# Gates of a product-key layer by one matmul per token, in groups of seven, with the low part added on VectorE

## The reference, cut to what matters

```python
best, pos = lax.top_k(cand, PEER_TOPK)
idx = jnp.take_along_axis(cand_idx, pos, axis=-1)
g = jax.nn.softmax(best, axis=-1)
u = expert_u[idx]
v = expert_v[idx]
a = jax.nn.gelu(jnp.einsum('td,thkd->thk', xb, u))
return jnp.einsum('thk,thkd->td', (g * a.astype(jnp.float32)).astype(v.dtype), v)
```

## Time and profile before

| | us |
|---|---|
| median of 3 runs | 4504.23 |
| lowest and highest | 4500.32, 4510.47 |
| the profiled execution | 4510.6 |
| its span on the core | 4508.9 |

### The profile page before, as it was taken

How to read it: one execution, slowest core, us unless ns; L and a number is a source line. 1 busy time by engine, 2 the same in 40 slices (tenths; PEclk the granted TensorE clock), 3 DMA queues, 4 the chain that set the end, 5 groups by cost and what they waited for, 6 DMA issues and landing times.

```text
span 4508.9 us, 79330 instructions
## 1 busy us (share of the span) xinstructions
PE 4158.0 (92%) x29440; PEld 3943.4 (87%) x29440; DVE 2733.9 (61%) x4379; ACT 1362.8 (30%) x2001; POOL 1002.1 (22%) x793
## 2 busy tenths in 40 slices
PE   4997988899999999999959979798999999999997
PEld 1785888899999999999838769798999999899997
DVE  1246547966766526777623565478667664277776
ACT  2221233233333333333222113332333333223332
POOL 0035000000122205555200630000001221245551
PEclk8998999999999999999979989999999999999998
DMA  4242221354445558999624422214444545589993
GB/s 142 98 114 107 85 80 61 94 164 136 125 170 180 187 185 309 343 346 341 231 94 131 108 100 83 71 66 135 140 136 147 173 171 204 166 316 349 346 350 147
DMA packets 304236, 781.05 MB, mean 173 GB/s; under 512 B 36352, under 2 KB 159616, under 8 KB 301488
## 3 DMA queue, kind: packets, MB, share of 16 engines
q1 hardware_dynamic: 187344, 483.65, 32.2%
q10 hardware_dynamic: 69600, 154.15, 9.3%
q0 software_dynamic: 47104, 141.00, 8.9%
HBM read 655.79 MB, written 122.88 MB: 173 GB/s over the span
## 4 chain that ended last, share of the span: by engine, by line
PE 80%; DVE 10%; DMA 3%; issue 3%; ACT 2%; another core or an unknown queue 1%; SPq 0%; DVEq 0%; ACTq 0%
PE pg L1318 16%; PE pg L1321 15%; PE pg L1319 15%; PE pm L1353 4%; PE pg L1566 4%; PE pg L1567 4%; PE pm L1567 4%; PE pg L1568 4%; PE pm L1568 4%; PE pm L1566 4%; PE pm L1527 4%; DMA raw<-stream 3%; DVE ys L1001 2%; DVE w_lo L842 1%
## 5 line engine op out<-in xcount | busy, mean ns | idle before, releaser
L1318 PE MATMUL pg<-a_hi,w_hi 128*128 128x260 f32 x6400 | 1706.5, 287 | 128.8 <-DVEq L873 40.6
L1319 PE MATMUL pg<-a_lo,w_hi 128*128 128x260 f32 x6400 | 1686.3, 285 | 0.0
L842 DVE TENSOR_TENSOR w_lo<-raw,w_hi 128x1024 fp32r<-128x1024 f32 x688 | 859.2, 1250 | 1306.2 <-ACT w_hi L751 750.3
L1318 PEld LDWEIGHTS pg<-a_hi,w_hi 128*128 128x128 f32 x6400 | 1226.7, 192 | 147.5 <-issue 110.7
L1321 PE MATMUL pg<-a_hi,w_lo 128*128 128x260 f32 x6400 | 1303.3, 286 | 0.5 <-issue 0.5
L1319 PEld LDWEIGHTS pg<-a_lo,w_hi 128*128 128x128 f32 x6400 | 1223.5, 191 | 0.4
L1321 PEld LDWEIGHTS pg<-a_hi,w_lo 128*128 128x128 f32 x6400 | 1000.4, 191 | 0.0
L751 ACT CAST w_hi<-raw 128x1024 fp32r<-128x1024 f32 x504 | 529.2, 1050 | 803.0 <-PE pm L1568 632.3
L500 POOL DMA_INDIRECT rows<-stream,at_v x256 | 280.5, 1096 | 829.0 <-issue 464.6
L549 ACT ACTIVATE hid<-pg 128x260 f32<-128x260 f32 x512 | 170.4, 385 | 956.7 <-PE pg L1321 953.2
L510 POOL TENSOR_TENSOR one_j<-one_j,g_lo 128x1024 fp32r<-128x1024 f32 x98 | 185.9, 1897 | 1080.9 <-DVEq L1221 1080.9
(11 more groups left out here) (221 smaller groups left out, 5856.1 us busy)
## 6 DMA issues: line engine op xcount, KB each, us to landing
raw<-stream SPq DMA_DIRECT2D x784, 512.0 KB
hidden_dram<-hid SPq DMA_DIRECT2D x256, 196.0 KB, 3.4
gate_dram<-gate_buf ACTq DMA_DIRECT2D x14, 3584.0 KB, 11.8
hid_in<-hidden_dram ACTq DMA_DIRECT2D x64, 784.0 KB
gate_in<-gate_dram ACTq DMA_DIRECT2D x64, 784.0 KB
hid_tok<-hid SPq DMA_DIRECT2D x256, 64.0 KB, 3.4
rows<-stream,at_v POOLq DMA_INDIRECT x256
hid_pick<-hid_tok,at_e POOLq DMA_INDIRECT x256
```

What stands on the lines that cost most here:

```text
L842: tt(ring(False, s), raw[:, s], ring(True, s).bitcast(F32), ALU.subtract).then_inc(lo_ready, 1)
L1318: pe.matmul(outs[h], w[0], a[h][0], start=first, stop=False)
L1319: pe.matmul(outs[h], w[0], a[h][1], start=False, stop=False)
```

## The change

A token's two matmuls of 128 columns become one of 256 columns: the high and the low part of `one_j` stand side by side as the moving operand, and the two results stand side by side in PSUM. So a token takes half a bank of `pm`, a group is seven tokens, and it fills seven of the eight halves of the four banks. There is room for one group only. The two results are added on the way out: ACT copies the high result to `gate_buf`, and DVE adds the low result from PSUM to it in place.

There are 56 groups instead of 49, in blocks 60 to 115. `gate_buf` has two halves of 28 tokens, each stored after four groups, with its own semaphore. The layout of `gate_buf` within a token group is unchanged in kind (experts outside, tokens inside), so both engines write one element in every 28; the copy before wrote runs of four. The copy on ACT stands at the start of the next block, ahead of the read of `hid`; the store is issued one block after the fourth group. The loads for the down stage move from block 113 to block 120.

```diff
-GS = 8
-GB = 56
+GS = 7
+GB = 28
...
-        gate_buf = sb(gs, "gate_buf", [P, NBLK, GB])
+        gate_buf = sb(gs, "gate_buf", [P, 2, NBLK, GB])
...
+        gate_parts = pm[:, :, :].rearrange("p b (t z j) -> p (b t) z j", t=2, z=2)
+
+        def gates_of(n):
+
+            m, k = divmod(n, GB // GS)
+            return gate_buf[:, m % 2, :, k * GS:(k + 1) * GS].rearrange("p j t -> p t j")
...
                 def take_gates(n):
+                    m, k = divmod(n, GB // GS)
                     act.wait_ge(g_prod, l * NSUB + (n + 1) + 2)
...
-                    for q in range(2):
-                        own.do(act.copy(gate_buf[:, :, t0 + 4 * q:t0 + 4 * q + 4],
-                                        pm[:, 2 * (n % 2) + q, :].rearrange("p (t j) -> p j t", t=4)))
-                    own.settle()
-                    act.sem_inc(g_free, 1)
...
+                    own.link(act.copy(gates_of(n), gate_parts[:, 0:GS, 0, :]))
+                    act.sem_inc(gate_hi_taken, 1)
+
+                def store_gates(m):
+                    act.wait_ge(g_free, l * NSUB + (m + 1) * (GB // GS) + 1)
+                    act.sem_inc(passed, 1)
+                    act.dma_start(gate_dram[m // 2][:, :, m % 2, :], gate_buf[:, m % 2].rearrange("p (g j) t -> p g (j t)", j=4)
+                                  ).then_inc(g_out[m % 2], 16)
...
+                    if G_FROM < block <= G_END:
+                        take_gates(block - G_FROM - 1)
                     act.wait_ge(hid_out[s], (l * (NBLK // 4) + block // 4) * 32 + 1)
...
-                    elif block < G_END:
-                        take_gates(block - G_FROM)
+                    if block - G_FROM - 1 in range(GB // GS, NSUB + 1, GB // GS):
+                        store_gates((block - G_FROM - 1) // (GB // GS) - 1)
...
+                def take_gates(n):
+                    dve.wait_ge(gate_hi_taken, l * NSUB + (n + 1))
+                    to = gates_of(n)
+                    own.link(tt(to, gate_parts[:, 0:GS, 1, :], to, ALU.add))
+                    dve.sem_inc(g_free, 1)
...
                         one_hots(block - G_FROM + 1)
+                    if G_FROM < block <= G_END:
+                        take_gates(block - G_FROM - 1)
                     split(l, T_EU + 4 + block, block % 4)
...
                     for t in range(GS):
-                        for z in range(2):
-                            mm = pe.matmul(pm[:, 2 * (n % 2) + t // 4, (t % 4) * P:(t % 4 + 1) * P], one_i[:, n % 2, t, :],
-                                           one_j[:, n % 2, z, t, :], start=z == 0, stop=z == 1)
+                        mm = pe.matmul(pm[:, t // 2, t % 2 * 2 * P:(t % 2 + 1) * 2 * P].rearrange("p (z j) -> p z j", z=2),
+                                       one_i[:, n % 2, t, :], one_j[:, n % 2, :, t, :], start=True, stop=True)
                     mm.then_inc(g_prod, 1)
```

More of the change, by code:

```diff
@@ L145, in build @@
     hidden_dram = nc.dram_tensor("hidden_dram", (P, NBLK, ND), F32).ap()
-    gate_dram = nc.dram_tensor("gate_dram", (GBN, P, NBLK, GB), F32).ap()
+    gate_dram = nc.dram_tensor("gate_dram", (GBN // 2, P, NBLK // 4, 2, 4 * GB), F32).ap()
     hid_tok = nc.dram_tensor("hid_tok", (P, NBLK, GT), F32).ap()
@@ L307, in build @@
         hid_out = [sem(f"hid_out{s}") for s in range(4)]
-        one_ready, g_prod, g_free, g_out = (sem(n) for n in ("one_ready", "g_prod", "g_free", "g_out"))
-        ghi_of_picks, one_lo_ready = sem("ghi_of_picks"), sem("one_lo_ready")
+        one_ready, g_prod, g_free = (sem(n) for n in ("one_ready", "g_prod", "g_free"))
+        g_out = [sem("g_out0"), sem("g_out1")]
+        ghi_of_picks, one_lo_ready, gate_hi_taken = sem("ghi_of_picks"), sem("one_lo_ready"), sem("gate_hi_taken")
         at_ready = sem("at_ready")
@@ L317, in build @@
         y_fin, y_done = sem("y_fin"), sem("y_done")
-        counts_from_one = [mod_taken, x_done, lo_ready, *pg_free, s_prod, s_copied, *hid_out, g_out, rt_ready, rt_prod, pm_clear]
-        counts_from_two = [g_free, g_prod]
+        counts_from_one = [mod_taken, x_done, lo_ready, *pg_free, s_prod, s_copied, *hid_out, *g_out, g_free, rt_ready, rt_prod, pm_clear]
+        counts_from_two = [g_prod]
         own_act, own_dve, own_pool = sem("own_act"), sem("own_dve"), sem("own_pool")
@@ L761, in load_group @@
                     act.dma_start(hid_to[:, :, :], hidden_dram[:, 4 * g:4 * g + 4, :]).then_inc(down_in[g % 3], 16)
-                    act.dma_start(gate_to[:, :, :], gate_dram.rearrange("b p j t -> p b (j t)")[:, :, 4 * g * GB:4 * (g + 1) * GB]
+                    act.dma_start(gate_to.rearrange("p (b z) x -> p b (z x)", z=2), gate_dram.rearrange("b p g z x -> p g b (z x)")[:, g]
                                   ).then_inc(down_in[g % 3], 16)
                 def take_gates(n):
+                    m, k = divmod(n, GB // GS)
                     act.wait_ge(g_prod, l * NSUB + (n + 1) + 2)
-                    if n % (GB // GS) == 0:
-                        act.wait_ge(g_out, (l * GBN + n // (GB // GS)) * 16 + 1)
-                    t0 = n % (GB // GS) * GS
-                    for q in range(2):
-                        own.do(act.copy(gate_buf[:, :, t0 + 4 * q:t0 + 4 * q + 4],
-                                        pm[:, 2 * (n % 2) + q, :].rearrange("p (t j) -> p j t", t=4)))
-                    own.settle()
-                    act.sem_inc(g_free, 1)
-                    if n % (GB // GS) == GB // GS - 1:
-                        act.sem_inc(passed, 1)
-                        act.dma_start(gate_dram[n // (GB // GS)].rearrange("p j t -> p (j t)"),
-                                      gate_buf[:, :, :].rearrange("p j t -> p (j t)")).then_inc(g_out, 16)
+                    if k == 0:
+                        act.wait_ge(g_out[m % 2], (l * (GBN // 2) + m // 2) * 16 + 1)
+                    own.link(act.copy(gates_of(n), gate_parts[:, 0:GS, 0, :]))
[5 more added lines that the diff above has]
+                                  ).then_inc(g_out[m % 2], 16)
                 for block in range(NBLK):
                     s = block % 4
+                    if G_FROM < block <= G_END:
+                        take_gates(block - G_FROM - 1)
                     act.wait_ge(hid_out[s], (l * (NBLK // 4) + block // 4) * 32 + 1)
@@ L802, in _ @@
                             act.sem_inc(ghi_of_picks, 1)
-                    elif block < G_END:
-                        take_gates(block - G_FROM)
+                    if block - G_FROM - 1 in range(GB // GS, NSUB + 1, GB // GS):
+                        store_gates((block - G_FROM - 1) // (GB // GS) - 1)
                     if block == G_END + 4:
-                        act.wait_ge(g_out, (l + 1) * (16 * GBN) + 1)
+                        for z in range(2):
+                            act.wait_ge(g_out[z], (l + 1) * (16 * GBN // 2) + 1)
                         for s in range(4):
@@ L1572, in _ @@
                 buffer(l, G_ED // 2, 1)
-                pe.wait_ge(g_free, (l + 1) * NSUB + 2)
+                pe.wait_ge(g_free, (l + 1) * NSUB + 1)
                 pe.sem_inc(passed, 1)
```

## The result

The changed kernel takes 4564.25 us (median of 4 runs, 4559.98 to 4566.90); the kernel before, on the same chip, 4502.27 us (4 runs, 4492.59 to 4510.47). The ratio is 1.0147, with a 95% interval of 1.0127 to 1.0166: slower by some 62 us. The forecast was 4508 us, practically no change, with 4486 to 4532 us as its own range and 4484 to 4562 us for 8 chances in 10; the measured time lies above both. The second rival, the strided add, had 4560 us.

The account below looks back on a forecast made before the run. PE bounds the gate blocks before; after, a DVE chain of 14.67 us over two blocks, 7.33 a block. That adds 1.8 us a layer, 3.6 for two, to 4504.2: 4508 us, range 4486 to 4532.

Parts of the forecast that it names:

- The second rival: DVE's strided add costs twice per element, 2.02 us; 28.1 us more per layer, 4560 us; chance 0.13.
- Step 5: DVE's new add in the chain: 896 elements with one source in PSUM, 1.09 us.
- The rest of the chain: Other terms between ACT's hid reads two blocks apart, through DVE and PE; whole chain 14.67 us, 7.33 a block.
- the low part of weights: On DVE, starts 1.97 us after ACT's read of hid, having waited for ACT's cast.
- one-hots: Three DVE instructions before the add, 3.22 us, then a gap of 0.22 us.
- seven wide matmuls: PE's gate matmuls of 256 columns, about 0.118 us each, 0.82 us for seven.
- PE's pause with the short add: PE idle before the gate matmuls, released by DVE, about 0.7 us per gate block on average.
- What was put at nothing: ACT's copy, POOL's multiply beside the add, the stores and the down-stage loads, all taken as covered at no cost.
- the start: First gate blocks: DVE begins with a backlog behind POOL and less room to recover; 0 to 3 us a layer, left out.
- The loads for the down stage: Issued at block 120 instead of 113, they need some 16 us and have 19; cover holds by 3 us.
- The third rival: PE's wide matmul is no faster than two narrow ones; 21.4 us more per layer, 4547 us; chance 0.05.
- the first: DVE keeps up and PE stays the gate blocks' bound at 6.60 us; 39.1 us less per layer, 4426 us; chance 0.09.

Follow-up runs that it names:

- e6: Changed kernel with six extra PE matmuls of 260 columns in each gate block, ahead of its wait, results overwritten; 4536.5 us, ratio 1.0104.
- e1: Changed kernel with gate_buf's element order changed so ACT and DVE write it without gaps (gates land in other places); 4492.12 us, ratio 1.0003.
- e7: Kernel before, with ACT's copies cut into pairs and singles and extra 896-element DVE adds at various strides after the gate blocks; 4493.5 us, one run.
- e5: Changed kernel without DVE's add, so gates lack their low part and ACT's copy frees pm; 4405.7 us, ratio 0.9810.
- e9: e8 with two matmuls of 128 columns per token instead of one of 256; 4492.4 us, ratio 0.9988.
- e8: e2 with DVE computing the low part of weights of block b-1 after the add in block b; 4416.2 us, ratio 0.9819.
- e2: Changed kernel, same gate_buf layout, but ACT and DVE walk it in runs of seven tokens, with jumps in PSUM; 4493.2 us, ratio 1.0008.
- e11: Changed kernel, strided gate_buf kept, with only the low part of weights of block b-1 moved after block b's add on DVE; 4431.2 us, ratio 0.9864.

## Why the prediction was wrong, by its own steps

**Step 5 was mis-sized.** It put the add at 1.09 us, and it took 1.90. With 1.90 in its place the prediction's own sum is 15.48 us for two blocks, 7.74 a block, 433.4 for the 56 blocks, 24.7 us a layer more than before. The run with the pauses filled has 25.2 and 25.1. The price of an element (1.04 ns) and the PSUM source were right: with plain writes the same add takes 1.091 us. What the add had in addition was the price of its stride in SBUF, 0.81 us (1.900 against 1.091). What failed was the sentence against the second rival. It took a row of eight elements at a stride (163 ns against 160) as evidence, though at eight elements a doubling would have been 8 ns, and it took ACT's old runs of four as near to runs of one. That row could not have shown the penalty; the second rival, at 0.13, deserved the first place or nearly so.

**The clock was not in the sum at all.** The prediction forecast PE's pauses but priced PE's work behind them at full clock, since the trace of before had 1.00 wherever PE was never idle. No rival named it either. That is 10 to 11.5 us a layer, some 22 in all (e6). Here the second rival, with 28.1 us a layer for a 2.02 us add, came near the measured median partly by luck: its 56 us are 7 too many for the add (24.7 a layer would have been enough), and it had neither the 22 us of the clock nor the some 10 us by which the medians (62) differ less than the two up stages (72). The profiled run of before lost twice that in its down stages; where its other runs lost theirs isn't shown.

**The rest of the chain held.** With the add at its forecast length (e1), the up stage is 2.1 us longer than before in each layer, where the prediction had 1.8, and the periods are 6.57 and 8.04 in turn, where it had 6.60 and 8.07 as one of two possibilities. Single terms: the low part of weights 1.93 to 2.00 us after the read of `hid` (1.97), one-hots 3.36 from the first to the add's start (3.44), seven wide matmuls 0.79 (0.82), PE's pause with the short add 0.62 a block (0.7).

**What was put at nothing cost nothing, but for the start.** POOL's multiply lies beside the add and neither is longer for it: with plain writes the add takes 1.091 us beside POOL in e1 and a plain add of the same size takes 1.085 without POOL in e7, and the multiply takes 1.69 us with the add beside it and without (e5). The stores of 448-byte runs land in 10.7 us (bounds 6 to 30). The copy on ACT, though 1.97 us long, is off the path (e5). The start was left out of the sum at 0 to 3 us, and it costs 2.8: the second gate block takes 10.84 us in e1 where its turn is 8.04. That the stage is still only 2.1 us longer has two reasons: the last two gate blocks take 6.57 us each, 1.5 us less than a turn, and the pairs between take 14.62 us instead of 14.67. The loads for the down stage, issued at 1673.37 and 1674.35, were used at 1692.44, and the first cast waits 3.05 us as before.

**The third rival falls** (e9 against e8), and **the first** would have been right only with a chain of 13.2 us or less; e8 gets there by another order (39.1 us less a layer).

What stays open: what exactly brings the clock down. The length of a pause alone doesn't decide it: in the changed kernel one of 1.79 us (to 1410.00) was followed by half clock, and those of 1.99 us (to 1348.31 and to 1443.78) were not; e1 and e8 have one of 2.5 and one of 1.35 us in the second gate block, the first followed by half clock, the second not. I have shown that filling the pauses takes the drop away, not which pause brings it.

## What to carry to other kernels

Before an instruction on hundreds of elements gets an access pattern, look which side of it has single elements at 16 bytes or more in SBUF, and turn the loops so that SBUF gets runs (seven elements here) and PSUM gets the jumps. When an added instruction makes an engine wait that never waited, write down the chain that leads back to it and look for what in it may come later: here moving one instruction that nobody was in a hurry for took 83 us from the two up stages with the quick add (e2 against e8) and 132 us with the slow one (after against e11), more than the 72 that the change had cost there. And where PE begins to pause, take it as one of the cases that its work behind the pause runs at half clock for a few microseconds.

## What the runs showed of the hardware that I had not expected

- DVE and ACT take 1.7 to 1.8 and 2.2 times as long when every one of 896 fp32 elements is on an SBUF line of its own: 1797 to 1955 ns against 1085 (DVE), 1965 against 905 (ACT). A strided read and a strided write together cost no more than one of them (1955 against 1865 and 1915).
- Reading every second fp32 element costs nothing (1085 ns); every fourth costs nearly as much as every seventh (1797 against 1865).
- From PSUM, single elements 1 KB apart cost DVE nothing (1092 ns against 1091) and ACT 9% (990 against 905).
- After 17 of 25 PE pauses of 1.76 to 2.01 us the granted clock was half for some 3.4 us, after 8 as long it stayed full; a kernel with 672 more matmuls in those pauses was faster by 10 to 11.5 us a layer.
